# A hybrid attention layer: deeper splitting, paired compression with its own buffers, compressed scores in column tiles, and the first heads turned on TensorE

## The reference

```python
h = rms_norm(x, norm_w)                      # x: (256, 2048)
proj = h @ w_in                              # 7704 columns: q, three k/v pairs, gates, z_a; q_b, k_b, v_b, z_b
# group A, 8 query heads in 2 groups, head width 128: three branches
k_cmp = silu(blocks(rope(k_c) + pos) @ cmp_k_w1) @ cmp_k_w2    # 15 overlapping blocks of 32 tokens, 4096 -> 512 -> 128
v_cmp = silu(blocks(v_c + pos) @ cmp_v_w1) @ cmp_v_w2
p_cmp = masked_softmax(q @ k_cmp.T * scale)  # scores over 15 compressed positions
o = g0 * (p_cmp @ v_cmp) + g1 * attention(q, k_s, v_s) + g2 * attention(q, k_w, v_w)
# group B: softmax(q1 k1) - lambda * softmax(q2 k2), times v, with a norm for each head
mixed = concat(o_a * silu(z_a), o_b * silu(z_b))
out = rms_norm(x + mixed @ w_out, final_norm_w)
```

## Time and profile before

| | |
|---|---|
| median of 3 runs | 512.49 us (511.84 to 513.07) |
| the profiled execution | 512.37 us |
| its span in the profile | 510.2 us |
| outside the span | 2.2 us |
| TensorE busy | 489.5 us, 96% of the span |
| VectorE busy | 364.2 us, 71% |
| ScalarE busy | 218.3 us, 43% |
| moved by the load queue and the others | 107.69 MB, 211 GB/s on average |

### The profile page before, as it was taken

How to read it: one execution, slowest core, us unless ns; L and a number is a source line. 1 busy time by engine, 2 the same in 40 slices (tenths; PEclk the granted TensorE clock), 3 DMA queues, 4 the chain that set the end, 5 groups by cost and what they waited for, 6 DMA issues and landing times.

```text
span 510.2 us, 6104 instructions
## 1 busy us (share of the span) xinstructions
PE 489.5 (96%) x2358; PEld 393.6 (77%) x2358; DVE 364.2 (71%) x513; ACT 218.3 (43%) x294; POOL 45.8 (9%) x41
## 2 busy tenths in 40 slices
PE   7999969999998999999999999999999998999993
PEld 6788845677765788888888888888888886888882
DVE  3855995448485899799798956667897978644532
ACT  5748112334331562354544544465444453334331
POOL 1003020002020301002020000002000000113030
PEclk9999989999999999999999999999999999999998
DMA  8998446887887864423344453524785562656005
GB/s 269 411 421 304 177 166 251 323 318 262 304 308 294 339 238 166 144 104 132 125 157 166 155 175 117 218 88 166 265 346 188 190 225 105 248 178 230 5 1 165
DMA packets 17868, 107.69 MB, mean 211 GB/s; under 512 B 2224, under 2 KB 2736, under 8 KB 5936
## 3 DMA queue, kind: packets, MB, share of 16 engines
q1 hardware_dynamic: 16544, 104.86, 55.6%
q10 hardware_dynamic: 1296, 2.44, 1.3%
HBM read 105.20 MB, written 2.10 MB: 210 GB/s over the span
## 4 chain that ended last, share of the span: by engine, by line
PE 67%; DVE 15%; DMA 8%; issue 5%; ACT 3%; POOL 1%; SPq 1%; POOLq 0%; DVEq 0%; ACTq 0%
PE acc L991 19%; PE acc L993 19%; PE acc L992 19%; DMA raw<-stream 8%; DVE wlo L638 4%; PE S L1117 3%; PE O L1031 2%; ACT whi L397 2%; DVE zT L691 1%; DVE qaT L691 1%; DVE kaT L691 1%; DVE kvcT L691 1%; PE S L1134 1%; DVE wlo L656 1%; PE S L1090 1%
## 5 line engine op out<-in xcount | busy, mean ns | idle before, releaser
L638 DVE TENSOR_TENSOR wlo<-raw,whi 128x2048 fp32r<-128x2048 f32 x72 | 165.9, 2308 | 99.0 <-ACT whi L397 98.5
L397 ACT ACTIVATE whi<-raw 128x2048 fp32r<-128x2048 f32 x72 | 138.0, 1918 | 167.5 <-PE acc L993 94.0
L991 PE MATMUL acc<-whi,hT_hi 128*128 128x512 f32 x432 | 172.4, 399 | 6.3 <-DVE wlo L638 5.8
L993 PE MATMUL acc<-whi,hT_lo 128*128 128x512 f32 x432 | 169.1, 391 | 0.0
L992 PE MATMUL acc<-wlo,hT_hi 128*128 128x512 f32 x432 | 169.0, 391 | 0.0
L991 PEld LDWEIGHTS acc<-whi,hT_hi 128*128 128x128 f32 x432 | 81.5, 189 | 35.3 <-issue 19.1
L993 PEld LDWEIGHTS acc<-whi,hT_lo 128*128 128x128 f32 x432 | 81.5, 189 | 17.5
L992 PEld LDWEIGHTS acc<-wlo,hT_hi 128*128 128x128 f32 x432 | 81.5, 189 | 16.3
L359 POOL TENSOR_TENSOR stage<-stage,stage 128x512 f32<-128x512 f32 (+1 forms) x16 | 24.9, 1571 | 194.8 <-DVE stage L682 194.8
L466 ACT ACTIVATE e<-S,small 128x128 f32<-128x128 f32 (+1 forms) x48 | 19.6, 421 | 28.4 <-DVE small L728 28.4
L691 DVE STREAM_TRANSPOSE zT<-stage 32x256 f32<-32x256 f32 x64 | 27.9, 436 | 2.0
(11 more groups left out here) (154 smaller groups left out, 510.5 us busy)
## 6 DMA issues: line engine op xcount, KB each, us to landing
raw<-stream SPq DMA_DIRECT2D x88, 1024.0 KB, 4.9
raw<-stream SPq DMA_DIRECT2D x6, 512.0 KB, 10.9
x_nat<-x_rows SPq DMA_DIRECT2D x2, 1024.0 KB, 14.1
x_nat<-x_rows SPq DMA_DIRECT2D x1, 2048.0 KB, 7.8
result<-x_nat SPq DMA_DIRECT2D x8, 256.0 KB, 3.2
xTs<-xT SPq DMA_DIRECT2D x3, 512.0 KB, 9.6
raw<-stream SPq DMA_DIRECT2D x4, 256.0 KB, 6.3
fw<-final_w ACTq DMA_DIRECT2D x1, 1024.0 KB, 5.8
```

Of the source, the lines that this page charges most:

```text
L397: act.activation(whi[:, n % SPLIT, :], raw[:, c % RAW, :], ACT.Copy).then_inc(hi_ready, 1)
L638: dve.tensor_tensor(wlo[:, n % SPLIT, :], raw[:, c % RAW, :], whi[:, n % SPLIT, :].bitcast(f32), ALU.subtract)\
L991: pe.matmul(acc_bank(n), xh, wh, start=k == 0, stop=False)
L993: last = pe.matmul(acc_bank(n), xl, wh, start=False, stop=k == KT - 1)
```

## The change

The diff has six parts.

- The order of the mixed stretch: compression chunks come in eight pairs, with pairs of "in" chunks between them: `in9, ck0, ck1, in10, in11, ck2, ck3, in12, in13, ...`, up to `in22, in23, cv6, cv7`. Chunks 0 to 9 and from 40 on keep their places.
- Compression chunks get two buffers of their own (`row_raw`, semaphores `row_in`); the four `raw` buffers serve the split chunks alone. SP's order becomes the list `LOADS`: the first two compression chunks behind chunk 8, then in turn some split chunks and the next pair. A pair's load waits until the pair before is used.
- Splitting looks ahead by two split chunks instead of two chunks of the stream, so compression chunks between don't count.
- `kvcT` is made by TensorE: `turn_kvc` runs 8 transposes behind the products of chunk 7, ScalarE copies them to SBUF (`take_kvc`, step 8). `kblkf` stays in step 8 of VectorE, `vblkf` moves to step 13. The 16 transposes on VectorE are gone.
- `cmp_scores` runs 32 matmuls a tile with 32 columns of weights each, in four column tiles, in place of 8 with 128 columns.
- In the last "in" block, `gate_ob` and the first half of `turn_z` come before the split of step 76; `cmp_keys` comes one chunk earlier.

```diff
-for _i in range(16):
-    STREAM += ([_in[9 + _i]] if _i < 2 else [_in[8 + _i]] if _i > 2 else []) + [_cmp[_i]]
+for _i in range(0, 16, 2):
+    STREAM += _in[9 + max(_i - 1, 0):10 + _i] + _cmp[_i:_i + 2]
...
-HEADS_AT = {b: 6 if b == 0 else LAST["in", b] + 2 for b in ROPE}
+HEADS_AT = {b: {0: 7, 5: LAST["in", b] + 3}.get(b, LAST["in", b] + 2) for b in ROPE}
...
-RAW, SPLIT = 4, 3
+RAW, SPLIT, ROW_RAW = 4, 3, 2
+LOADS = HALVED[RAW:9] + ROWS[:ROW_RAW]
+for _i in range(0, len(ROWS), ROW_RAW):
+    _n = sum(c < ROWS[_i] for c in HALVED) + RAW + 1
+    LOADS += [c for c in HALVED[:_n] if c >= RAW and c not in LOADS] + ROWS[_i + ROW_RAW:_i + 2 * ROW_RAW]
+LOADS += [c for c in HALVED[RAW:] if c not in LOADS]
...
-            for c in range(RAW, N_CHUNKS):
-                before = c - RAW
-                if before in PLACE:
-                    sp.wait_ge(hi_ready, PLACE[before] + 1)
-                    sp.wait_ge(lo_ready, PLACE[before] + 1)
-                else:
-                    wait_used(sp, before)
+            for c in LOADS:
+                if c in ROW_PLACE:
+                    m = ROW_PLACE[c]
+                    if m >= ROW_RAW:
+                        wait_used(sp, ROWS[m - ROW_RAW])
+                    sp.dma_start(row_raw[:, m % ROW_RAW, :], stream[c, :, :]).then_inc(row_in[m % ROW_RAW], 16)
+                    continue
+                n = PLACE[c]
+                sp.wait_ge(hi_ready, n - RAW + 1)
+                sp.wait_ge(lo_ready, n - RAW + 1)
...
-                elif c + 2 in PLACE:
-                    split_hi(c + 2)
+                elif c in PLACE and PLACE[c] + 2 < len(HALVED):
+                    split_hi(HALVED[PLACE[c] + 2])
...
+            def take_kvc():
+                for t in range(TT):
+                    act.wait_ge(kvc_turned, t + 1)
+                    act.activation(kvcT[:, :, t * P:(t + 1) * P], S[:, 1 + t, :].rearrange("p (h q) -> p h q", h=4), ACT.Copy)\
+                        .then_inc(kvc_taken, 1)
...
+                    if b == 5:
+                        dve.wait_ge(hid_done, 2)
...
+                if c == LAST["in", Z[-1]] + 1:
+                    gate_ob(Z[-1])
+                    turn_z(Z[-1], range(0, 2))
...
-                if c == 8:
-                    dve.wait_ge(heads_turned, turned(0))
-                    dve.wait_ge(blk_zero, 2)
-                    for k, w in enumerate(("ck", "cv")):
+                for k, w in enumerate(("ck", "cv")):
+                    if c == (8, 13)[k]:
+                        dve.wait_ge(kvc_taken, TT)
+                        dve.wait_ge(blk_zero, 2)
...
+            def turn_kvc():
+                pe.wait_ge(const_in, 32)
+                for t in range(TT):
+                    pe.wait_ge(rope_ready, t + 1)
+                    pe.wait_ge(acc_read["s"], t + 1)
+                    for h in range(4):
+                        last = pe.transpose(S[:, 1 + t, h * P:(h + 1) * P], stage[:, t, h * P:(h + 1) * P], ident)
+                    last.then_inc(kvc_turned, 1)
...
-                    last = pe.matmul(S[:, 0, (8 * t + h) * NC:(8 * t + h + 1) * NC], qaT[:, h, t * P:(t + 1) * P],
-                                     kcmpT[:, (h // 4) * NC:(h // 4 + 1) * NC], start=True, stop=True)
+                    for i in range(4):
+                        last = pe.matmul(S[32 * i:32 * (i + 1), 0, (8 * t + h) * NC:(8 * t + h + 1) * NC],
+                                         qaT[:, h, t * P + 32 * i:t * P + 32 * (i + 1)],
+                                         kcmpT[:, (h // 4) * NC:(h // 4 + 1) * NC], start=True, stop=True,
+                                         tile_position=(0, 32 * i))
...
-                if c == K_END + 3:
+                if c == K_END + 2:
                     cmp_keys()
```

More of the change, by code:

```diff
@@ L66 @@
 PLACE = {c: i for i, c in enumerate(HALVED)}
+ROWS = [c for c, s in enumerate(STREAM) if s[0] in ("ck", "cv")]
+ROW_PLACE = {c: i for i, c in enumerate(ROWS)}
 ROPE = [0, 1, 3, 4, 5, 6, 7, 8]
-HEADS_AT = {b: 6 if b == 0 else LAST["in", b] + 2 for b in ROPE}
+HEADS_AT = {b: {0: 7, 5: LAST["in", b] + 3}.get(b, LAST["in", b] + 2) for b in ROPE}
 Z = [11, 12, 13, 14]
@@ L216, in program @@
         raw_in = [sem(f"raw_in{i}") for i in range(RAW)]
+        row_in = [sem(f"row_in{i}") for i in range(ROW_RAW)]
         hi_ready, lo_ready = sem("hi_ready"), sem("lo_ready")
@@ L547, in _ @@
                     start(c + 2)
-                elif c + 2 in PLACE:
-                    split_hi(c + 2)
+                elif c in PLACE and PLACE[c] + 2 < len(HALVED):
+                    split_hi(HALVED[PLACE[c] + 2])
                 if c == 4:
                     act.dma_start(gwf[:, :, :], w_gate).then_inc(gw_in, 16)
+                if c == HEADS_AT[0] + 1:
+                    take_kvc()
                 if c == 7:
@@ L637, in split_lo @@
                 dve.wait_ge(hi_ready, n + 1)
-                dve.tensor_tensor(wlo[:, n % SPLIT, :], raw[:, c % RAW, :], whi[:, n % SPLIT, :].bitcast(f32), ALU.subtract)\
+                dve.tensor_tensor(wlo[:, n % SPLIT, :], raw[:, n % RAW, :], whi[:, n % SPLIT, :].bitcast(f32), ALU.subtract)\
                     .then_inc(lo_ready, 1)
@@ L669, in rope @@
                 f = SCALE if b in Q_BLOCKS else 1.0
-                if n:
+                if n > 1:
                     dve.wait_ge(heads_turned, turned(ROPE[n - 1]))
+                elif n:
+                    dve.wait_ge(kvc_turned, t + 1)
                 else:
@@ L857, in _ @@
                     start(c + 2)
-                elif c + 2 in PLACE:
-                    split_lo(c + 2)
+                elif c in PLACE and PLACE[c] + 2 < len(HALVED):
+                    split_lo(HALVED[PLACE[c] + 2])
                 if c + 2 == RELOAD:
                     dve.wait_ge(x_in, 16 * TT + 16)
-                if c == 8:
-                    dve.wait_ge(heads_turned, turned(0))
-                    dve.wait_ge(blk_zero, 2)
-                    for k, w in enumerate(("ck", "cv")):
+                if c == LAST["in", Z[-1]] + 2:
+                    turn_z(Z[-1], range(2, 4))
+                for k, w in enumerate(("ck", "cv")):
+                    if c == (8, 13)[k]:
+                        dve.wait_ge(kvc_taken, TT)
+                        dve.wait_ge(blk_zero, 2)
                         src = bass.AP(kvcT, kvcT[:, 2 * k:2 * k + 2, :].offset,
@@ L926, in _ @@
                         take_ob(u)
-                for b in ROPE:
+                for b in ROPE[1:]:
                     if c == HEADS_AT[b]:
@@ L932, in _ @@
                 for b in Z:
-                    if c == Z_AT[b]:
-                        if b >= 13:
+                    if c == Z_AT[b] and b < Z[-1]:
+                        if b == 13:
                             gate_ob(b)
                         turn_z(b, range(0, 2))
-                    if c == Z_AT[b] + 1:
+                    if c == Z_AT[b] + 1 and b < Z[-1]:
                         turn_z(b, range(2, 4))
@@ L1026, in products_cmp @@
                 k = 0 if kind == "ck" else 1
-                pe.wait_ge(raw_in[c % RAW], 16 * (c // RAW))
+                m = ROW_PLACE[c]
+                pe.wait_ge(row_in[m % ROW_RAW], 16 * (m // ROW_RAW + 1))
                 if j == 0:
@@ L1032, in products_cmp @@
                                      blkf[kind][:, CH * j + i, :, :].rearrange("p g n -> p (g n)"),
-                                     raw[:, c % RAW, i * NB:(i + 1) * NB], start=j == 0, stop=j == CMP_BLOCK // CH - 1,
+                                     row_raw[:, m % ROW_RAW, i * NB:(i + 1) * NB], start=j == 0, stop=j == CMP_BLOCK // CH - 1,
                                      tile_position=(0, 32 * i))
@@ L1190, in _ @@
                     products(c, after_tile=cmp_scores if c == CMP_SCORES_AT else None)
+                if c == HEADS_AT[0]:
+                    turn_kvc()
                 if c == GATE_AT:
```

17 lines of the change are left out of this document (9 added, 8 removed).

## The result

The changed kernel takes 498.12 us (median of 4 runs, 497.8 to 498.4) against 512.43 us before (4 runs, 511.84 to 513.07): a ratio of 0.9731, 95% interval 0.9712 to 0.9751. The forecast was 499.2, its range 497.0 to 503.5. Run again later it took 498.08 against 512.25.

The account below looks back on a forecast made before the run. TensorE, busy 489.5 of 510.2 us, was taken as the bound. Terms for start, transposes, buffers, pairs, scores and end summed to -13.2 us, from the profiled 512.37 to 499.2 us; range 497.0 to 503.5.

Parts of the forecast that it names:

- up to chunk 40: stops, clock, transposes, loads, pairs: Start through mixed stretch: -3.8 -1.7 -0.6 -0.6 for stops and clock, +1.0 transposes, -1.4 buffers, -2.4 pairs.
- compressed scores, two tiles: Four column tiles loading side by side take each tile from 1.8 to 0.8 us: -2.0, bounds -2.1 to +0.6.
- end of the inputs: Earlier gating and turning of the last z block remove TensorE's wait for `mixB_lo` before chunk 79: -1.7 us, without margin.
- The stop at 70.76: TensorE waits 3.79 us for the split of chunk 11 because VectorE is late; a 0.50 clock follows for 3.41 us.
- the whole 6.7 us of the start: The 3.79 us stop, 1.7 of slow clock, and waits of 0.60 and 0.58 all go with VectorE relieved.
- The pairs: Mixed stretch: seven fewer changeovers there and back at 0.34 us each, -2.4 us; bounds nothing to 2.4.
- Rival B: Column tiles bring nothing in the compressed scores, 0 to 0.6 us worse: 501.2 to 501.8 us; chance 0.16.
- the floor of 25 ns: The skill's least distance between matmul starts: 64 records would need 1.6 us a tile, so no gain in the scores.
- The round of one load: Compressed scores: a round over four column tiles costs one load, 0.03 us, so 16 rounds take 0.5 us a tile.
- SP's blocking: In-order SP queue: a pair's load stands before later "in" loads, but these are needed some 24 us later; costs nothing.
- D: SP's queue starves the splits as each pair's load blocks "in" loads behind it: 525 to 538 us; chance 0.04.
- -1.4 for the buffers: Own buffers and deeper splitting remove TensorE's 1.36 us wait at 158.29, where ScalarE had waited 6.01 for a load.

Follow-up runs that it names:

- singles_look_two: Changed kernel with the old stream order (single compression chunks) and the old lookahead of two stream chunks, own buffers kept: 503.38 us.
- singles_shared_look_two: Kernel before with only first heads on TensorE, compressed scores in column tiles and the new order at the end of the inputs: 505.77 us.
- tiles_beside_pairs: Changed kernel with three more small products in four column tiles, all but one turn of hidden rows directly before a pair: 496.02 us.
- look_two_chunks: Changed kernel splitting two chunks of the stream ahead again instead of two split chunks: 515.88 us.

## Why the prediction was right, point by point

| step | forecast | measured |
|---|---|---|
| up to chunk 40: stops, clock, transposes, loads, pairs | -9.5 | 171.60 to 161.68: -9.9 |
| compressed scores, two tiles | -2.0 | 1.81 and 1.70 to 0.66 and 0.67: -2.2 |
| end of the inputs | -1.7 | chunk 76 to 79, 18.16 to 16.32: -1.8 |
| all | -13.2 | profiled execution 512.37 to 498.40: -14.0 |

Rows behind the table, next to the earlier trace rows and those above; first the kernel before, then the changed one:

```profile
171.60 0.50 PE L991 MATMUL acc<-whi,hT_hi 128*128 128x512 f32 x1
...
190.97 0.48 PE L991 MATMUL acc<-whi,hT_hi 128*128 128x512 f32 x1
...
193.81 1.85 PE L1090 MATMUL S<-kcmpT,qaT 128*128 128x16 f32 x16
195.51 1.14 PE L1078 MATMUL O<-w2v,hidT 128*128 128x128 f32 x8
...
412.49 0.39 PE L991 MATMUL acc<-whi,mixA_hi 128*128 128x512 f32 x1
```

```profile
182.68 0.74 PE L1133 MATMUL S<-kcmpT,qaT 128*32 128x16 f32 x64
183.35 1.16 PE L1120 MATMUL O<-w2v,hidT 128*128 128x128 f32 x8
...
400.35 0.39 PE L1022 MATMUL acc<-whi,mixA_hi 128*128 128x512 f32 x1
...
416.67 0.39 PE L1022 MATMUL acc<-whi,mixB_hi 128*128 128x512 f32 x1
```

Each part gave a little more than its forecast, 0.8 us in all. The other 0.3 of the 1.1 us between 499.2 and 498.12 is that the changed kernel's profiled execution (498.40) was slower than its median.

**The stop at 70.76** was VectorE's lateness, as read from the earlier trace rows. Undoing that part alone brings a stop of 2.92 us and a fallen clock, +3.7 us in the median. But the relief alone is not enough: with the old lookahead a stop of 1.76 us comes up near 77 us instead, for a split behind the turning of block 1 (`singles_look_two`, `singles_shared_look_two`). The sum had the whole 6.7 us of the start under the transposes; the deeper splitting has a share in them. The transposes cost 0.8 us (53.81 - 53.01) where I took 1.0. The first compression chunk starts 66.62 - 64.87 = 1.75 us behind the gate products' start, against 65.90 - 63.80 = 2.10 before; I had put that in the range, not in the sum.

**The pairs**: 2.4 us forecast, 2.4 to 2.5 by undoing them.

**The scores**: 1.8 by undoing them, 2.2 in the trace. Rival B and the floor of 25 ns fell: records start 9 ns apart on average. The round of one load that I had taken held: 16 rounds in 0.56 us are 0.035 us each, against 0.03.

**The end**: 1.6 by undoing it. I had seen no margin; there were 0.6 us, since `gate_ob` of the first tile needn't wait for the second tile's SiLU: `mixB_lo` is ready at 416.03 and needed at 416.67.

**The buffers**: SP's blocking cost nothing (D fell), as worked out. But "-1.4 for the buffers" gave the right sum for a part whose cover I had not priced. I had named the stall that the buffers take away and not what deeper splitting and pairs would cost without them: 16.2 us more. For the lookahead alone I had no term, and before its run I held it for worth nothing; with pairs it is worth 17.8 us. That these costs stay out of the changed kernel was not worked out, so in this the sum was lucky. The heads, scores and end are worth 6.5 us together (512.25 to 505.77). The other three are worth 7.7, and only together: on that base the deeper splitting alone makes it 16.4 slower, own buffers alone 2.4 faster, both 5.2 faster. So the changed kernel stands on two conditions that the sum didn't show: deeper splitting needs the own buffers, and pairs need the deeper splitting.

What stays open: the corner of pairs with shared buffers and the old lookahead was not run, nor were `cmp_keys` a chunk earlier and the wait for `hid_done` undone by themselves. Undoing the scores costs 1.8 in the median, while its own trace shows 2.1 more in the two tiles (1.70 each against 0.66 and 0.67) and the trace of the kernel before 2.2. That execution reached them 0.4 us earlier, and it ran in the session in which the kernel before was fastest.

## What to carry to other kernels

When one engine is busy 96% of the span, read its list of waits, the granted clock behind each, and the distance between starts; a sum of these few terms came within 1.1 us of 498.1. When parts of a change share a queue, price each also with the others absent: an engine's step that waits for data holds up all that is written behind it, so looking further ahead pays only where the data can be there. And a small float32 product with 16 to 32 moving columns took the time of its weight loads here. Cutting it into column tiles, interleaving the tiles and putting it beside other tiled work gained 1.8 us in the scores and 2.1 in `tiles_beside_pairs`.

## What the runs showed of the hardware

Records of a float32 matmul in four column tiles, 16 columns moving, start 9 ns apart on average when the tiles alternate and 27 ns apart when eight matmuls in a row use one tile; with 128 columns of weights they start 0.11 us apart. The page "TensorE: Matmul & The Clock Gate" of the Trainium skill, section "Wait — 56ns, not 53.3ns?", gives about 25 ns as the least distance; the run with alternating tiles doesn't agree. The run with one tile in a row doesn't go against it, but can't bear it out either: 27 ns is also what the prediction worked out for a load of 32 columns, 28 ns.

The same stop seems to cost more in some runs than in others, with what the clock does behind it. `singles_look_two` took 502.50 and 502.52 us at a mean clock of 0.994 (the second is the profiled one, with a stop of 1.76 us and a full clock behind it), and 504.25 and 504.39 at 0.991. `look_two_chunks`, with five stops, took 512.79 us at 0.992 and 518.76 at 0.979. The kernel before took 510.25 us at 0.993 and 513.18 at 0.988. The mean clock of a run doesn't say it all: `singles_shared_look_two` took 505.24 us at 0.990, but 506.31 at 0.994. The changed kernel has no such stop: its eight runs lie between 497.71 and 498.40. So the spread narrowed with the time.
